# Two attentions that divide their values instead of their probabilities, and hand gated, split rows on

## The chip, the core and the metric

The kernel runs on one NeuronCore of a Trainium2 chip. The metric is the device time of one execution in microseconds (us), as the median of several runs. Its engines are PE (matmuls and transposes, into PSUM), DVE, ACT and POOL (elementwise work; POOL doesn't read PSUM here) and SP, whose queue issues most DMAs. Each engine runs its own list in order; they meet through semaphores and wait for one another at the end of each block.

## What is computed

The program is a first transformer block (latent attention, differential attention, routed experts), which the change doesn't touch, and a second block of two layers on a sequence of 1024 with width 1024 and 16 heads of 64. Cut to its two attentions:

```python
# layer 1: forgetting attention
logits = q @ k.T * scale + c[:, None] - c[None, :]        # c: running sum of log forget gates
p = softmax(where(causal, logits, -inf))
o = p @ v
h = h + (o * silu(gate)) @ w_out_a
# layer 2: window of 128 keys, 4 key/value heads, one sink logit a head
probs = softmax(concatenate([logits, sink], -1))[..., :-1]
o = probs @ v_band
h = h + (o * silu(gate)) @ w_out_b
```

All is f32. The output projections are made of three f32r products of split operands: x = hi + lo, x_hi is the cast of x to f32r, x_lo = x - x_hi, and hi·hi + hi·lo + lo·hi is summed (`split_product`, lines 329 to 331).

## The kernel before

Memory is a row of 16 KiB slots; a name such as `oh_a` or `wo_a` is a tile at a slot, and `_rest` is the low part, written over its source.

**First attention (`phase_fox`, 64 pairs).** A pair p is a pair of heads c = p // 8 and a query tile t = p % 8 of 128 rows; its keys are the t + 1 tiles up to the diagonal. So a pair's cost grows with t and starts over every eight pairs. PE's list has in step p: transposes of the probabilities of pair p-3 (first four key tiles), a mask matmul and the scores of pair p, the value product of pair p-4, and the remaining transposes of pair p-3 (only for t of 4 and more). DVE adds the gate row C and takes the maximum (L2531), ACT does exp with the row sum (L2492), DVE the reciprocal (L2539), POOL multiplies every probability in place by the reciprocal (L2503), and then PE may transpose (L2562). The transposed tiles go from PSUM to `fox_pt`: the first four key tiles by ACT (L2480), the rest by DVE (L2517), through three PSUM banks in turn. The value product (L2601) writes a quarter of bank 7, transposed: head dimension down, queries across. ACT copies the bank to `qa` (L2486) after every fourth pair, and the product of the next pair waits for that.

**Output projection (`phase_gated_out`).** It begins after a barrier. For the first layer SP loads both halves of the weights, `wo_a`, and then H; for the second they were loaded during the attention. DVE multiplies the attention output by the gate G in eight pieces of 1024 columns (L2682), ACT casts it (L2659), DVE subtracts (L2686). ACT casts the weights (L2657, L2663), POOL subtracts the first half (L2674), DVE the second (L2691). PE waits for four output pieces and a whole weight half, then runs 16 units of 24 matmuls; DVE adds each to H (L2700).

**Window attention (`phase_window`, 32 units).** A unit is one key/value head j, of four query heads, and one query tile b; b = 0 has half the keys. PE in step u: mask (L3146) and scores (L3151) of unit u, transposes of u-3 (L3163), value product of u-4 (L3175). DVE: maximum (L3116) and four small operations, reciprocal (L3126), and both copies of transposed tiles (L3134, L3135). ACT: four exps (L3088) and the copy of the values to `qb` (L3096). POOL scales the probabilities (L3075).

## Time and profile before

| | us |
|---|---|
| median of 3 runs (2932.11 to 2933.54) | 2932.21 |
| the profiled execution | 2931.2 |
| its span in the trace | 2929.0 |

| engine | busy us | share of the span |
|---|---|---|
| PE | 2510.2 | 86% |
| DVE | 1702.3 | 58% |
| ACT | 1353.0 | 46% |
| POOL | 639.6 | 22% |

In the profile times are from the start of the span. The first attention runs from 1997.8 to 2295.6, its output projection until about 2414, the window attention from 2686.2 to 2816.9, the last projection to the end. A matmul's record ends some 0.27 us after PE could issue the next (the drain); an idle time in brackets stands ahead of the row, with what ended it; "x20" counts merged instructions. An f32 matmul that isn't a transpose has two records.

### The profile page before, as it was taken

Reading aid. Unit: us, or ns where it says so; the run is one execution under the profiler, and the core shown is the slowest. Engines: PE = TensorE matmul, PEld = TensorE weight load, DVE = VectorE, ACT = ScalarE, POOL = GpSimd, SP = SyncE. Lnnn points to the kernel's source line nnn. Section 1 sums busy time; section 2 is a strip of 40 time slices with the busy share of each in tenths; the row PEclk is TensorE's granted clock in tenths of the full one; section 3 lists DMA queues with packets and bytes.
Section 4 is the critical chain, followed back from the end, with each engine's and each line's share of the span. In section 5 each row is a group of like instructions: output and inputs, shape, how many; then the busy total and the mean of one; then the engine's idle time right before and its main releaser. Section 6 shows DMA issues by size and latency. Waiting matters only on the chain. (4 is left out here: it accounts for less than half of the span.)

```text
span 2929.0 us, 37676 instructions
## 1 busy us (share of the span) xinstructions
PE 2510.2 (86%) x13381; PEld 2013.9 (69%) x13381; DVE 1702.3 (58%) x2888; ACT 1353.0 (46%) x2358; POOL 639.6 (22%) x515
## 2 busy tenths in 40 slices
PE   1899799999975999999941999997888597998969
PEld 1787279788764888888831878885655476886547
DVE  5662655687336999999937145412444616742981
ACT  2243144696124888888834233323565304222540
POOL 0121012230101211111112000004777400002950
PEclk9899899999967999999975999998999798999989
DMA  6542000002027999999944211043000312114101
GB/s 221 173 129 62 0 1 1 1 30 87 0 74 323 409 415 417 412 412 410 410 161 179 78 44 59 22 137 115 30 30 16 116 58 87 29 47 156 57 8 51
DMA packets 126925, 400.22 MB, mean 137 GB/s; under 512 B 11947, under 2 KB 62256, under 8 KB 114370
## 3 DMA queue, kind: packets, MB, share of 16 engines
q1 hardware_dynamic: 113726, 354.07, 31.7%
q0 software_dynamic: 12048, 42.56, 3.7%
q8 instruction: 89, 1.46, 0.2%
q10 hardware_dynamic: 1012, 1.72, 0.2%
q14 instruction: 50, 0.41, 0.0%
HBM read 347.93 MB, written 50.40 MB: 136 GB/s over the span
## 5 line engine op out<-in xcount | busy, mean ns | idle before, releaser
L2503 POOL TENSOR_SCALAR fox_l<-fox_l,stat 128x256 f32<-128x256 f32 (+7 forms) x128 | 219.0, 1726 | 76.0 <-DVE stat L2539 76.0
L2531 DVE CUSTOM_DVE_ANT_0 fox_l<-PS,fox_c 128x256 f32<-128x256 f32 (+7 forms) x128 | 92.1, 756 | 156.3 <-PE PS L2585 111.2
L2492 ACT ACTIVATE fox_l<-fox_l,stat 128x256 f32<-128x256 f32 (+7 forms) x128 | 98.3, 770 | 75.3 <-DVE stat L2531 75.3
L3075 POOL TENSOR_SCALAR win_p<-win_p,stat 128x256 f32<-128x256 f32 (+1 forms) x128 | 110.7, 887 | 20.0 <-DVE stat L3126 20.0
L2562 PE MATMUL PS<-mats,fox_l 128*128 128x128 f32 x576 | 89.7, 291 | 25.8 <-POOL fox_l L2503 17.6
L329 PE MATMUL PS<-wehg,xsTh 128*128 128x512 f32 x256 | 100.4, 392 | 8.3 <-DVE we0g_rest L1888 6.9
L329 PE MATMUL PS<-wehd,aTh 128*128 128x512 f32 x256 | 100.5, 392 | 6.6 <-DVE aTl L1907 6.6
L329 PE MATMUL PS<-wqkh,uTh 128*128 128x512 f32 x256 | 103.3, 403 | 0.0
L329 PE MATMUL PS<-wehu,xsTh 128*128 128x512 f32 x256 | 102.9, 402 | 0.0
L331 PE MATMUL PS<-wqkh,uTl 128*128 128x512 f32 x256 | 100.5, 392 | 0.0
L331 PE MATMUL PS<-wehd,aTl 128*128 128x512 f32 x256 | 100.2, 391 | 0.0
L331 PE MATMUL PS<-wehg,xsTl 128*128 128x512 f32 x256 | 100.2, 391 | 0.0
L331 PE MATMUL PS<-wehu,xsTl 128*128 128x512 f32 x256 | 100.1, 391 | 0.0
L330 PE MATMUL PS<-wqk_rest,uTh 128*128 128x512 f32 x256 | 100.0, 391 | 0.0
L2562 PEld LDWEIGHTS PS<-mats,fox_l 128*128 128x128 f32 x576 | 64.3, 145 | 49.8 <-POOL fox_l L2503 40.6
L2700 DVE TENSOR_TENSOR H<-PS,H 128x512 f32<-128x512 f32 x32 | 21.9, 691 | 126.7 <-PE PS L331 126.6
L2601 PEld LDWEIGHTS PS<-fox_pt,va 128*64 128x64 f32 x1152 | 64.1, 140 | 39.4 <-ACT fox_pt L2480 36.4
L2601 PE MATMUL PS<-fox_pt,va 128*64 128x128 f32 x1152 | 79.9, 285 | 11.9 <-ACT qa L2486 10.9
L451 PE MATMUL PS<-mats,xn_na 128*128 128x128 f32 x64 | 11.5, 364 | 91.6 <-DVE xn_na L413 91.6
L1210 DVE TENSOR_REDUCE stat<-PS 128x1 f32<-128x1024 f32 x64 | 78.0, 1224 | 18.9 <-PE PS L1247 15.7
L329 PE MATMUL PS<-hTh,winh 128*128 128x512 f32 x208 | 83.2, 400 | 6.7 <-DVE win_rest L603 6.7
L2854 POOL DMA_DIRECT2D g_dram<-b_sg x16 | 8.7, 544 | 354.3 <-ACT b_sg L2909 354.3
(569 smaller groups left out, 7794.8 us busy)
## 6 DMA issues: line engine op xcount, KB each, us to landing
we0g<-in_w_expert_gate SPq DMA_DIRECT2D x16, 2048.0 KB, 11.1
we0u<-in_w_expert_up SPq DMA_DIRECT2D x16, 2048.0 KB, 9.6
we1g<-in_w_expert_gate SPq DMA_DIRECT2D x16, 2048.0 KB, 11.3
we0d<-in_w_expert_down SPq DMA_DIRECT2D x16, 2048.0 KB, 10.5
we1u<-in_w_expert_up SPq DMA_DIRECT2D x16, 2048.0 KB, 9.7
we1d<-in_w_expert_down SPq DMA_DIRECT2D x16, 2048.0 KB, 10.6
wada_rest<-in_w_ada SPq DMA_DIRECT2D x16, 1024.0 KB, 5.2
wada<-in_w_ada SPq DMA_DIRECT2D x4, 2048.0 KB, 13.5
```

The source lines that it names most:

```text
L329: nc.tensor.matmul(out, lh, rh, start=start, stop=False)
L330: nc.tensor.matmul(out, lh, rl, start=False, stop=False)
L331: return nc.tensor.matmul(out, ll, rh, start=False, stop=stop)
L451: last = nc.tensor.transpose(PS[:, u % NB, j * P:(j + 1) * P], xn[:, j, k * P:(k + 1) * P], env.ident)
L1210: nc.vector.reduce_max(nb[:, w % 4:w % 4 + 1], bank(w), AX_X, negate=True).then_inc(nb_ready, 1)
L2492: nc.scalar.activation(prob(p, e)[:, 0:K], prob(p, e)[:, 0:K], ACT.Exp, bias=nbm[:, u % 8:u % 8 + 1], scale=-1.0, accum_out=rsum[:, u % 8: ...
L2503: nc.gpsimd.tensor_scalar(prob(p, e)[:, 0:K], prob(p, e)[:, 0:K], rsum[:, u % 8:u % 8 + 1], None, ALU.mult).then_inc(p_ready, 1)
L2531: nc.vector.tensor_tensor_reduce(out=prob(p, e)[:, 0:K], in0=PS[:, 2 * e:2 * e + 2, :].rearrange("p a b -> p (a b)")[:, 0:K], in1=C[:, h % ...
L2562: last = nc.tensor.transpose(PS[:, 4 + at % NTB, (k % 4) * P:(k % 4 + 1) * P], prob(v, e)[:, k * P:(k + 1) * P], env.ident)
L2601: last = nc.tensor.matmul(PS[e * HD:(e + 1) * HD, 7, (t % 4) * P:(t % 4 + 1) * P], env.va[:, k, h * HD:(h + 1) * HD], PT[:, w % 2, e, k, : ...
L2700: nc.vector.tensor_tensor(H[:, t, h], PS[:, u % 8, :], H[:, t, h], ALU.add).then_inc(h_done, 1)
L3075: last = nc.gpsimd.tensor_scalar(p, p, rs[:, c + i:c + i + 1], None, ALU.mult)
```

## The change

It does three things in both attentions. First, probabilities are transposed and multiplied with the values undivided. POOL instead copies the two (window: four) reciprocals of a pair over 64 columns a head (`rx`), PE transposes this tile, and it lands in the same PSUM bank beside the value sums, laid out as they are; DVE multiplies the two. In the first attention it first copies the turned reciprocals to SBUF, and does this for two pairs at once, after every odd pair; in the window it first multiplies them by the gate. Second, the gate, the cast and the subtraction of the attention output move from the projection into the attention, onto POOL (window: the gate onto DVE). Third, the projection takes ready rows. The first half of `wo_a` is loaded while the first attention runs, all weight casts are ACT's and all weight subtractions DVE's, and PE waits for weight pieces one by one. In the window the copies of transposed tiles go from DVE to ACT, as one instruction, and ACT's copy of the values goes away. G of the window comes in four loads.

```diff
+    nbm, rsum = env.stat[:, 0:8], env.stat[:, 8:24]
...
+    def rx(w):
+        at = (2 + w // 2 % 2) * P
+        return env.pad[w % 2][:, at:at + P]
...
+                if h == NH // 2 + 2:
+                    sp.wait_ge(s_ready, NPAIR)
+                    load(sp, env.wo_a[0:1])
...
-                w = p - LAG - 2
-                if w >= 0 and w % 4 == 3:
-                    c, n = w // T, w % T // 4
-                    act.wait_ge(pv_done, w + 1)
-                    nc.scalar.copy(env.qa[:, c, n * HALF:(n + 1) * HALF], PS[:, 7, :]).then_inc(o_out, 1)
...
-            for p in range(NPAIR if scale_on_pool else 0):
...
+            for p in range(NPAIR + LAG + 2):
+                if p < NPAIR:
+                    at = 2 * p % 16
                     pool.wait_ge(r_ready, p + 1)
-                    nc.gpsimd.tensor_scalar(prob(p, e)[:, 0:K], prob(p, e)[:, 0:K], rsum[:, u % 8:u % 8 + 1], None,
-                                            ALU.mult).then_inc(p_ready, 1)
+                    if p >= 4:
+                        pool.wait_ge(pv_done, p - 3)
+                    nc.gpsimd.tensor_copy(rx(p).rearrange("p (e d) -> p e d", e=2),
+                                          rsum[:, at:at + 2].unsqueeze(2).to_broadcast([P, 2, HD])
+                                          ).then_inc(rx_ready, 1)
+                w = p - LAG - 2
+                if w < 0 or w % 2 == 0:
+                    continue
+                i = w // 2
+                o = two(env.qa, w)
+                if i == 0:
+                    pool.wait_ge(g_in, 16)
+                pool.wait_ge(o_out, i + 1)
+                nc.gpsimd.tensor_tensor(o, o, two(g, w), ALU.mult).then_inc(gated, 1)
+                pool.wait_ge(gated, i + 1)
+                nc.gpsimd.tensor_copy(two(Oh, w), o).then_inc(o_hi, 1)
+                pool.wait_ge(o_hi, i + 1)
+                nc.gpsimd.tensor_tensor(two(Ol, w), o, two(Oh, w).bitcast(F32), ALU.subtract).then_inc(o_lo, 1)
...
-            for p in range(NPAIR + LAG + 1):
+            for p in range(NPAIR + LAG + 2):
+                w = p - LAG - 2
+                if w >= 0 and w % 2:
+                    rb = env.pad[w // 2 % 2][:, 0:2 * P]
+                    dve.wait_ge(pv_done, w + 1)
+                    if w >= 4:
+                        dve.wait_ge(o_out, w // 2 - 1)
+                    nc.vector.tensor_copy(rb, PS[:, 7, 2 * P:4 * P]).then_inc(rb_out, 1)
+                    dve.wait_ge(rb_out, w // 2 + 1)
+                    nc.vector.tensor_tensor(two(env.qa, w), PS[:, 7, 0:2 * P], rb, ALU.mult).then_inc(o_out, 1)
...
-                    pe.wait_ge(p_ready, 2 * v + e + 1)
+                    pe.wait_ge(exp_done, 2 * v + e + 1)
...
+                    pe.wait_ge(rx_ready, w + 1)
+                    if w >= 2:
+                        pe.wait_ge(o_out, w // 2)
+                    nc.tensor.transpose(PS[:, 7, (2 + w % 2) * P:(3 + w % 2) * P], rx(w), env.ident)
                     pe.wait_ge(pt_first, 2 * w + 2)
...
-                    if w >= 4:
-                        pe.wait_ge(o_out, w // 4)
...
-                            last = nc.tensor.matmul(PS[e * HD:(e + 1) * HD, 7, (t % 4) * P:(t % 4 + 1) * P],
+                            last = nc.tensor.matmul(PS[e * HD:(e + 1) * HD, 7, (w % 2) * P:(w % 2 + 1) * P],
...
-            load(sp, wo_loads)
+            load(sp, loads)
...
+            for j in range(8):
+                act.wait_ge(wo[j // 4][1], 16)
+                nc.scalar.copy(wpiece(woh, j), wpiece(raw, j)).then_inc(w_hi, 1)
...
-            for j in range(4):
...
+            for j in range(8):
                 dve.wait_ge(w_hi, j + 1)
...
+                nc.vector.tensor_tensor(wpiece(wl, j), wpiece(raw, j), wpiece(woh, j).bitcast(F32), ALU.subtract
+                                        ).then_inc(w_lo, 1)
...
-                if n == 0:
-                    pe.wait_ge(o_lo, 4 * (t // 4) + 4)
...
-                pe.wait_ge(w_lo2 if n else w_lo, 4)
+                    if t == 0 and k % 2 == 0:
+                        pe.wait_ge(w_lo, 4 * n + k // 2 + 1)
...
+            for j in range(KVH):
+                sp.dma_start(g[:, 2 * j:2 * j + 2, :], env.g_dram.rearrange("(k p) s -> p k s", p=P)[:, 2 * j:2 * j + 2, :]
+                             ).then_inc(g_in[j], 16)
+            load(sp, env.wo_b)
...
-            for v in range(NU):
-                f = first(units[v][1])
-                pool.wait_ge(r_ready, v + 1)
-                for i in range(G):
-                    p = Pb[:, v % 4, i, f:]
-                    last = nc.gpsimd.tensor_scalar(p, p, rs[:, c + i:c + i + 1], None, ALU.mult)
-                last.then_inc(p_ready, 1)
+            for u in range(NU + 5):
+                if u < NU:
+                    at = 4 * (u % 8)
+                    pool.wait_ge(r_ready, u + 1)
+                    if u >= 2:
+                        pool.wait_ge(o_ready, u - 1)
+                    nc.gpsimd.tensor_copy(rx(u).rearrange("p (c e d) -> p c e d", c=2, e=2),
+                                          rs[:, at:at + 4].rearrange("p (e c) -> p c e", e=2).unsqueeze(3)
+                                          .to_broadcast([P, 2, 2, HD])).then_inc(rx_ready, 1)
+                w = u - 5
+                if w >= 0:
+                    pool.wait_ge(o_out, w + 1)
+                    nc.gpsimd.tensor_copy(block_of(Oh, w), block_of(env.qb, w)).then_inc(o_hi, 1)
+                    pool.wait_ge(o_hi, w + 1)
+                    nc.gpsimd.tensor_tensor(block_of(Ol, w), block_of(env.qb, w), block_of(Oh, w).bitcast(F32),
+                                            ALU.subtract).then_inc(o_lo, 1)
...
+                v = u - 3
+                if v >= 0:
+                    f = 1 if units[v][1] == 0 else 0
+                    act.wait_ge(t_ready, v + 1)
+                    if v >= 2:
+                        act.wait_ge(o_ready, v - 1)
+                    nc.scalar.copy(PT[v % 2][:, f:, :], PS[:, 4 + f:6, :]).then_inc(pt_ready, 1)
...
-                w = u - 4
-                if w >= 0:
-                    act.wait_ge(o_ready, w + 1)
-                    nc.scalar.copy(env.qb[:, 2 * j:2 * j + 2, b * P:(b + 1) * P],
-                                   PS[:, 6 + w % 2, 0:2 * P].rearrange("p (c q) -> p c q", c=2)).then_inc(oo_act, 1)
...
-                        dve.wait_ge(o_ready, v - 1)
-                    if units[v][1]:
-                        nc.vector.tensor_copy(PT[v % 2][:, 0, :], PS[:, 4, :])
-                    nc.vector.tensor_copy(PT[v % 2][:, 1, :], PS[:, 5, :]).then_inc(pt_dve, 1)
...
+                w = u - 5
+                if w >= 0:
+                    dve.wait_ge(o_ready, w + 1)
+                    if w % T == 0:
+                        dve.wait_ge(g_in[w // T], 16)
+                    do(nc.vector.tensor_tensor(rg(w), PS[:, 6 + w % 2, 2 * P:4 * P].rearrange("p (c q) -> p c q", c=2),
+                                               block_of(g, w), ALU.mult))
+                    nc.vector.tensor_tensor(block_of(env.qb, w),
+                                            PS[:, 6 + w % 2, 0:2 * P].rearrange("p (c q) -> p c q", c=2), rg(w), ALU.mult
+                                            ).then_inc(o_out, 1)
...
-                    pe.wait_ge(p_ready, v + 1)
+                    pe.wait_ge(exp_done, v + 1)
-                        pe.wait_ge(pt_dve, v)
+                        pe.wait_ge(pt_ready, v)
...
+                    pe.wait_ge(rx_ready, w + 1)
+                    if w >= 2:
+                        pe.wait_ge(o_out, w - 1)
+                    for c in range(2):
+                        nc.tensor.transpose(PS[:, 6 + w % 2, (2 + c) * P:(3 + c) * P], rx(w)[:, c * P:(c + 1) * P], env.ident)
+                    pe.wait_ge(pt_ready, w + 1)
...
+    env.G, env.O_a = gates("a", 3), (m.at("oh_a", 3, [P, KD, S], F32R), m.rest("qa"))
+    env.wo_a = out_weights("a", (7, 9), A["w_out_a_2"][0])
...
+    phase_gated_out(nc, A, env, sem, "a", env.O_a, env.wo_a, env.wo_a[1:], (8, 10), H, sem("h_in_a"),
+                    env.h_dram, [env.ha_dram], extra=trig)
...
+    env.Gb, env.Gb_in = m.at("G_b", 3, [P, KD, S]), [sem(f"G_in_b{j}") for j in range(KVH)]
+    env.wo_b, env.h_in_b = out_weights("b", (5, 6), A["w_out_b_2"][0]), sem("h_in_b")
+    env.O_b = m.at("oh_b", 3, [P, KD, S], F32R), m.rest("qb")
...
+    phase_gated_out(nc, A, env, sem, "b", env.O_b, env.wo_b, [], (7, 8), H, env.h_in_b, None, [out])
```

## Rows read from the trace of the kernel before

**Rows 1.** Busy time by stretch: us, PE, PEld, DVE, ACT, POOL, clock, DMA
```profile
1997.80:2295.60 297.80, 249.89 (x2240) 171.12 (x2240) 125.53 (x384) 168.62 (x401) 219.05 (x128) 0.95 0.12 44
...
2686.20:2816.90 130.70, 113.69 (x800) 65.92 (x800) 111.80 (x284) 72.96 (x320) 110.67 (x128) 0.98 0.26 97
```

**Rows 2.** Waits in the first attention: engine, releaser, us, times, longest
```profile
DVE fox_l L2531 <- PE PS L2585: 111.2, 56, 2.9
...
PEld PS L2562 <- POOL fox_l L2503: 40.6, 58, 1.8
...
PE PS L2601 <- ACT qa L2486: 10.9, 8, 1.8
```

**Rows 3.** Timeline of one head pair: the mask matmul opening a score step
```profile
2102.30 0.28 PE L2579 MATMUL PS<-masksb,identb 128*128 128x128 bf16 x2
...
2107.18 0.28 PE L2579 MATMUL PS<-masksb,identb 128*128 128x128 bf16 x2
...
2112.82 0.28 PE L2579 MATMUL PS<-masksb,identb 128*128 128x128 bf16 x2
...
2117.22 0.28 PE L2579 MATMUL PS<-masksb,identb 128*128 128x128 bf16 x2
...
2132.21 0.28 PE L2579 MATMUL PS<-masksb,identb 128*128 128x128 bf16 x2
...
2137.69 0.28 PE L2579 MATMUL PS<-masksb,identb 128*128 128x128 bf16 x2
```

**Rows 4.** Timeline, same pair: what PE waited for, and a releasing copy
```profile
2104.29 1.31 PE L2601 MATMUL PS<-fox_pt,va 128*64 128x128 f32 x20 [1.30 <-ACT qa L2486]
...
2112.33 0.66 PE L2562 MATMUL PS<-mats,fox_l 128*128 128x128 f32 x4 [1.54 <-POOL fox_l L2503]
...
2136.80 0.47 DVE L2517 COPY fox_pt<-PS 128x128 f32<-128x128 f32 x2
...
2137.22 0.63 PE L2562 MATMUL PS<-mats,fox_l 128*128 128x128 f32 x4 [0.99 <-DVE fox_pt L2517]
```

**Rows 5.** Timeline at the end of the first attention
```profile
2278.52 10.67 POOL L2503 TENSOR_SCALAR fox_l<-fox_l,stat 128x896 f32<-128x896 f32 x4 [0.44 <-DVE stat L2539]
...
2295.59 0.59 ACT L2486 COPY qa<-PS 128x512 f32<-128x512 f32 x1 [5.07 <-PE PS L2601]
```

**Rows 6.** Groups by form, first attention: count, busy us, mean ns
```profile
L2531 DVE CUSTOM_DVE_ANT_0 fox_l<-PS,fox_c 128x256 f32<-128x256 f32 x16 | 6.2, 423 | 11.5 <-PE PS L2585 11.5
```

**Rows 7.** Timeline from the first attention into its output projection
```profile
2296.49 2.36 DVE L2682 TENSOR_TENSOR qa<-qa,G_a 128x1024 f32<-128x1024 f32 x2 [3.00 <-PEq L2458]
...
2306.28 1.04 ACT L2657 CAST woh_a<-wo_a 128x1024 fp32r<-128x1024 f32 x1 [10.10 <-DMA wo_a<-in_w_out_a]
...
2310.77 3.36 DVE L2682 TENSOR_TENSOR qa<-qa,G_a 128x1024 f32<-128x1024 f32 x1
...
2324.16 0.80 PE L329 MATMUL PS<-woh_a,oh_a 128*128 128x512 f32 x1 [28.60 <-DVE qa_rest L2686]
...
2332.04 4.62 DVE L2691 TENSOR_TENSOR wo_a_rest<-wo_a,woh_a 128x1024 fp32r<-128x1024 f32 x4
```

**Rows 8.** Timeline of POOL in an earlier stage: a cast, a two-input pass
```profile
510.15 1.04 POOL L959 CAST dif_kh<-dk 64x1024 fp32r<-64x1024 f32 x1 [11.57 <-ACT dif_kh L987]
511.27 2.35 POOL L961 TENSOR_TENSOR dif_kz<-dk,dif_kh 64x1024 fp32r<-64x1024 f32 x1
```

**Rows 9.** Second attention: three mask matmuls; ACT's and DVE's forms
```profile
2740.39 0.60 PE L3146 MATMUL PS<-masksb,identb 128*128 128x512 bf16 x2
...
2744.03 0.39 PE L3146 MATMUL PS<-masksb,identb 128*128 128x256 bf16 x2
...
2774.55 0.39 PE L3146 MATMUL PS<-masksb,identb 128*128 128x256 bf16 x2
...
L3088 ACT ACTIVATE win_p<-PS,stat 128x256 f32<-128x256 f32 x112 | 51.6, 473 | 44.0 <-DVE stat L3120 44.0
...
L3135 DVE COPY win_pt<-PS 128x512 f32<-128x512 f32 x32 | 21.7, 679 | 0.0
```

**Rows 10.** Timeline: the second output projection's first matmul
```profile
2836.60 0.79 PE L329 MATMUL PS<-woh_b,oh_b 128*128 128x512 f32 x1 [19.71 <-DVE qb_rest L2686]
```

More of the change, by code:

```diff
@@ L2467, in _ @@
                     load(sp, [env.G])
+                if h == NH // 2 + 2:
+                    sp.wait_ge(s_ready, NPAIR)
+                    load(sp, env.wo_a[0:1])
         @block.scalar
         def _(act):
-            for p in range(NPAIR + LAG + 2):
+            for p in range(NPAIR + LAG):
                 v = p - LAG
@@ L2653, in _ @@
         def _(act):
-            for i in range(NP_):
-                if i < 4:
-                    act.wait_ge(halves[0][1], 16)
-                    nc.scalar.copy(wpiece(woh, i), wpiece([x[0] for x in halves], i)).then_inc(w_hi, 1)
-                act.wait_ge(gated, i + 1)
-                nc.scalar.copy(piece(Oh, i), piece(O, i)).then_inc(o_hi, 1)
-            act.wait_ge(halves[1][1], 16)
-            for j in range(4, 8):
-                nc.scalar.copy(wpiece(woh, j), wpiece([x[0] for x in halves], j)).then_inc(w_hi, 1)
+            for j in range(8):
+                act.wait_ge(wo[j // 4][1], 16)
+                nc.scalar.copy(wpiece(woh, j), wpiece(raw, j)).then_inc(w_hi, 1)
             if extra is not None:
@@ L3053, in four, with rx, rg, block_of @@
         return PS[:, 2 * (u % 2):2 * (u % 2) + 2, :].rearrange("p a (i k) -> p (a i) k", i=2)
[L3055 to L3057 removed]
+    def rx(w):
+        return env.pad[w % 2][:, 2 * P:4 * P]
+    def rg(w):
+        return env.pad[w % 2][:, 0:2 * P].rearrange("p (c q) -> p c q", c=2)
+    def block_of(x, w):
+        j, b = units[w]
+        return x[:, 2 * j:2 * j + 2, b * P:(b + 1) * P]
     with nc.Block() as block:
@@ L3104, in do @@
                 dve.wait_ge(dve_step, step.mark(instruction))
-            for u in range(NU + 3):
+            for u in range(NU + 5):
                 if u < NU:
@@ L3207, in second_block @@
     del taken[:]
-    env.G = gates("a", 3)
+    env.c_in = [sem(f"c_in{i}") for i in range(4)]
+    env.C = m.at("fox_c", 11, [P, 4, S])
+    env.G, env.O_a = gates("a", 3), (m.at("oh_a", 3, [P, KD, S], F32R), m.rest("qa"))
+    env.wo_a = out_weights("a", (7, 9), A["w_out_a_2"][0])
     phase_fox(nc, A, env, sem)
```

130 lines of the change are left out of this document (41 added, 89 removed).

## The prediction

> **What bounds the kernel now.** I began with the busy time in stretches [rows 1]. The change touches two attention stages and the hand-over from each to its output projection, and these differ in kind. In the first attention (297.8 us) PE is busy for 249.9 us by modelled ends, POOL for 219.1 and no engine is full. The waits there [rows 2] show PE held for POOL, which scales every probability tile in place ahead of its transposes, and for ACT's evacuation of the value sums. In the 28.6 us behind it PE does nothing at all [rows 7]. The second attention has POOL busy for 110.7 of 130.7 us and PE for 113.7; behind it lies another gap of 19.7 us [rows 10]. So each part has to be read by itself: a loop of dependences, a plain gap, a nearly full PE, and a second gap.
>
> **First hand-over, the largest term.** ACT's last evacuation starts at 2295.59, just as the last value product ends [rows 5]; the first projection matmul starts at 2324.16 after 28.60 us of idle PE [rows 7]. Between them lie the wait for the weights (the first cast starts at 2306.28, 10.10 us of it on the DMA), then gating, casting and subtracting of the whole attention output. POOL subtracts the weights at the same time; DVE's product takes 3.36 us then. In the new kernel the first weight half is in SBUF already and the output rows are gated and split inside the attention. What is left behind the last value product is:
> - DVE copies 256 columns of turned reciprocals out of PSUM and multiplies. The nearest row is a DVE pass over 256 PSUM columns, 0.423 us [rows 6]; two of them and a semaphore step are 0.9.
> - POOL gates, casts and subtracts 256 columns. POOL's two-input pass over 1024 columns takes 2.35 us and its cast 1.04 [rows 8]. By columns that is 0.6 + 0.26 + 0.6; with 0.1 a step for start and semaphore I take 1.9. The bounds are 1.5 (by columns) and 5.7 (the full 1024-column prices).
> - The barrier between blocks: ACT's last copy ends at 2296.18 and DVE starts the next block at 2296.49, 0.3 [rows 5, 7].
> - The first piece of weights: a cast of 1.04 us, then a DVE subtraction, four of which take 4.62 us [rows 7]. With its semaphore steps this is 2.5.
>
> Together 5.6 us in place of 28.6: **-23 us**. Later pieces come every 1.2 us, and PE needs at least 1.4 us for the six matmuls of a piece, so it isn't starved. The new load of the second half is wanted only eight units later: the 16 additions to H of this block follow PE, not the load. PE started out of a long idle stretch before too, so I book nothing for its clock.
>
> **Second hand-over.** The gap is 19.71 us [rows 10]. The new tail is shorter, since DVE gates here: 0.9 (DVE), a cast and a subtraction of 256 columns on POOL, 1.1, then 0.3 and 2.5 as above: 4.8. **-15 us**.
>
> **First attention's loop.** Its period is one pair of heads: 2102.30 to 2137.69, 35.39 us, repeated [rows 3]. I walk it by the starts of the mask matmuls, each of which opens a score step. PE issues in order, so the step length is what stood in its way:
> - Step t=0, 4.88 us. The value product at 2104.29 had waited 1.30 us for ACT's copy of a full bank [rows 4]. That wait goes, and 0.29 us for POOL; one more transpose is added. The transposes that follow one another run at 0.11 us each (four of them read 0.66 us with the drain of 0.27 [rows 4]). About 3.4.
> - Step 1, 5.64 us. PE stood 1.54 us for POOL at 2112.33 [rows 4]. Without it DVE's new copy and product, 0.9 us, stand ahead of the second PSUM evacuation that frees the transposes' bank. So the gain is 1.5 and not 1.9 with the ACT wait: 4.1.
> - Step 2, 4.40 us: its product waited 0.55 us behind the late transposes; with one transpose more, 4.0.
> - Steps 3 to 6, 14.99 us together [rows 3]. These are set by scores, then DVE's logits pass, then the next scores, and DVE has 1 to 2 us of slack in them for its new pair. 14.9.
> - Step 7, 5.48 us, gets **longer**. DVE finishes the longest logits pass, and its copy at 2136.80 is what releases PE at 2137.22 (0.99 us of wait) [rows 4]. The new copy and product stand in front of it in DVE's queue: 5.5 + 0.9 = 6.4.
>
> Sum 32.8, that is 2.6 less for each of seven periods: -18. The first period has no POOL wait to lose but gets the 0.9, +0.6. The drain was ruled by POOL, which had 10.67 us of scaling still queued at 2278.52 [rows 5]; following the same queues without it I get the last product 3 us sooner. **-20.5** in all. Unknown here is the order in which DVE's new pair meets its waits. If it costs 0.9 at every even step instead of two, four times eight, the gain is 20.5 - 14 = 6. If it hides everywhere, it is 20.5 + 14 = 34; steps 3 to 6 give nothing either way.
>
> POOL's work in this loop falls from 27 us in a period to about 10: eight broadcast copies of 128 columns and four chains of three instructions. The broadcast copies are needed three steps later. POOL's wait on the gate chain holds only the next such copy, with that slack. The added waits on `pv_done` are for a buffer last used four pairs earlier. The SP queue stops at head 10 until half the scores are done; behind it is the row of head 11, wanted one period (33 us) later, and the 2 MB weight load ahead of it took 10 us in [rows 7]. I book nothing.
>
> **Second attention's loop.** Period of eight units: 2744.03 to 2774.55, 30.52 us [rows 9]. A step in which PE waits for nothing is 3.64 us (2740.39 to 2744.03). Eight of these, less 1.5 for the first block with half the keys, are 27.6: PE idles 2.9. Two added transposes a unit, 0.22, give 29.3. ACT gives up its 0.38 us copy of the values and takes DVE's two copies as one of 1024 columns: about 1.0 with four exponentials of 0.47 and their accumulator reads [rows 9] makes 3.1 a unit, under 3.7. DVE, at 111.8 / 32 = 3.5 us a unit [rows 1], loses two copies of 0.68 [rows 9] and gains 0.9. So PE is the bound and the gain is 30.5 - 29.4 = 1.1 for each of three periods, -3.4, and 2 us in the drain, where POOL and DVE no longer stand between the last transposes and their products: **-5.4**. Bounds: +4 if each pair of transposes also costs a drain of 0.17 and the old idle time stays, -9 if the idle time goes in the first period too.
>
> **Sum.** 23 + 15 + 20.5 + 5.4 = 64 us. The profiled execution took 2931.2 us (its span 2929.0 and 2.2 around it), 1.0 under the median of 2932.2. 2931.2 - 64 = 2867, and about 2868 by the median.
>
> **Rivals.**
> 1. *DVE becomes the link in the first loop.* The new copy and product lengthen every even step, and what POOL's waits gave is taken back: -6 instead of -20.5. For it: step 7 shows that DVE's copies do release PE. Against: in steps 4 and 6 DVE waits for PE (111 us over the stage [rows 2]). Time 2868 + 14.5 = 2883; 2889 if nothing at all is left.
> 2. *The transposes cost more in the window stage.* PE is nearly full there, so an added switch or a late reciprocal goes straight through: +4 instead of -5.4, time 2878.
> 3. *DVE slack in the first loop is larger than I read*, and the new pair hides at steps 1 and 7 too: 2868 - 14 = 2854.
> 4. *Slower than before: POOL and DVE exclude one another.* A DVE pass with both inputs in SBUF takes 1.2 us by itself (four in 4.62) and took 3.36 beside a POOL subtraction [rows 7]. In the window stage DVE has some 3.1 us of work a unit and POOL 2.0; run strictly one after the other, with 0.1 us for each of nine semaphore steps, they make 6.0 us a unit against 3.8. That is 32 x 2.2 = +70, and with it the 5.4 isn't gained: 2931 - 64 + 5 + 70 = 2942. It turns slower from 5.8 us a unit on. Against it: the first attention's DVE passes over PSUM keep their length (0.423 us mean over 16) with POOL busy almost all the time [rows 6, 1].
>
> The Trainium skill, "SBUF — State Buffer", section "Who interferes with whom", calls the shared ports an exclusive lock, but says that a DVE instruction with at most one SBUF input, outside the two-port modes, doesn't contend with GpSimd; both new DVE passes read PSUM for the other input, so by that rule rival 4 falls away, and by the lock taken without the exception it would stand. The rows of the first attention agree with the exception.
>
> **How the numbers follow.** Forecast 0.62 (2860 to 2876); rival 1, 0.18; rival 2, 0.08; rival 3, 0.07; rival 4, 0.05. The likeliest is 2868. For 8 in 10 the range takes in rivals 1 to 3 and their combination, 2851 to 2894, leaving out rival 4 and the far tails. A measurement can tell 0.2%, 6 us, from no change. All cases but rival 4 are faster by far more: faster 0.94, within 0.2% 0.01, slower 0.05.
>
> **What would show each step.** The PE idle ahead of the first matmul of each projection: near 5.6 and 4.8 us, released by a DVE subtraction of weights and not by one of attention rows. The period of the first loop near 33 us, with step 7 near 6.4 and no wait of PE on POOL's scaling; if it is 35, rival 1. The window's period near 29.4, PE's idle under 0.5 a unit. POOL's three new instructions of 256 columns at 0.7, 0.3 and 0.7 us; over 1.5 each would say rival 4. The prediction fails most cheaply in the hand-overs: if the projection's first matmul waits on something I took as ready (the barrier behind POOL, the weight half, a queue of POOL's gates that is units behind), each microsecond there counts in full.

## The result, and the profile after

The changed kernel takes 2877.54 us (2876.0 to 2881.6), against 2932.88 us for the kernel before on the same chips: a ratio of 0.9815, with a 95% interval of 0.9803 to 0.9826. That is 55 us less, where 64 had been worked out. Its profiled execution has a span of 2875.5 us, 53.5 less than before.

I cut both spans at the same six events (first mask matmul and last value product of each attention, first matmul of each output projection) and take differences:

| part | worked out | measured |
|---|---|---|
| first hand-over (PE idle) | 28.60 to 5.6: -23 | 28.60 to 5.68: -22.9 |
| second hand-over | 19.71 to 4.8: -15 | 19.71 to 6.47: -13.2 |
| first attention, loop and drain | -20.5 | -10.9 |
| second attention, loop and drain | -5.4 | -7.4 |
| all that lies ahead of, between and behind | 0 | +1.0 |
| sum | -64 | -53.4 |

The 1.0 is 1.2 us by which the first attention starts later, behind code that the change doesn't touch. In the other kernels below that start lies anywhere from 1997.3 to 2003.1 us, so differences of a few us between whole runs are read by stages, not by spans.

Busy time of the changed kernel by stretch, columns as in [rows 1]: first attention, first gap, second attention, second gap.
```profile
1999.06:2285.83 286.77, 259.60 (x2304) 174.84 (x2304) 149.22 (x446) 163.11 (x385) 75.03 (x157) 0.96 0.15 53
2285.83:2291.50 5.67, 0.00 (x0) 0.00 (x1) 2.13 (x4) 2.36 (x3) 3.68 (x6) 0.78 0.19 42
2653.36:2776.58 123.22, 120.02 (x864) 72.86 (x864) 89.21 (x286) 94.47 (x321) 43.77 (x90) 0.98 0.27 103
2776.58:2783.05 6.47, 0.01 (x1) 0.00 (x0) 2.12 (x4) 2.35 (x3) 3.55 (x7) 0.81 0.00 0
```
POOL's busy time falls from 219 to 75 us in the first attention. In the second PE is now busy for 120.0 of 123.2 us.

The first hand-over, timeline of all engines from the last value product to the first projection matmul. It answers to [rows 7].
```profile
2285.86 0.42 DVE L2539 COPY pad<-PS 128x256 f32<-128x256 f32 x1 [2.15 <-PE PS L2629]
2286.32 0.42 DVE L2541 TENSOR_TENSOR qa<-PS,pad 128x256 f32<-128x256 f32 x1
2286.82 0.72 POOL L2524 TENSOR_TENSOR qa<-qa,G_a 128x256 f32<-128x256 f32 x1 [5.97 <-DVE qa L2541]
2287.61 0.40 POOL L2526 CAST oh_a<-qa 128x256 fp32r<-128x256 f32 x1
2288.09 0.72 POOL L2528 TENSOR_TENSOR qa_rest<-qa,oh_a 128x256 fp32r<-128x256 f32 x1
2289.14 3.88 ACT L2674 CAST woh_a<-wo_a 128x1024 fp32r<-128x1024 f32 x4 [8.52 <-PEq L2469]
...
2290.22 2.36 DVE L2687 TENSOR_TENSOR wo_a_rest<-wo_a,woh_a 128x1024 fp32r<-128x1024 f32 x2 [3.48 <-ACT woh_a L2674]
...
2291.50 0.79 PE L329 MATMUL PS<-woh_a,oh_a 128*128 128x512 f32 x1 [5.68 <-DVE wo_a_rest L2687]
```
This is the chain of the prediction, link by link: 0.9 us on DVE, 2.0 on POOL (1.9 had been taken), 0.3 for the barrier, 2.4 for the first piece of weights. ACT finds the weights landed.

One period of the first loop, PE's timeline, cut to the mask matmuls that open steps 0 to 4, step 7 and the next period, and to what PE waited for. It answers to [rows 3, 4].
```profile
2101.99 0.27 PE L2605 MATMUL PS<-masksb,identb 128*128 128x128 bf16 x2
2102.19 0.49 PE L2611 MATMUL PS<-ka,qa 64*128 64x128 f32 x4
2102.61 0.33 PE L2622 MATMUL PS<-mats,pad 128*128 128x128 f32 x1
2102.87 1.31 PE L2629 MATMUL PS<-fox_pt,va 128*64 128x128 f32 x20
...
2105.62 0.28 PE L2605 MATMUL PS<-masksb,identb 128*128 128x128 bf16 x2
...
2109.79 0.63 PE L2588 MATMUL PS<-mats,fox_l 128*128 128x128 f32 x4 [0.30 <-DVE fox_pt L2550]
2110.26 0.28 PE L2605 MATMUL PS<-masksb,identb 128*128 128x128 bf16 x2
...
2114.91 0.28 PE L2605 MATMUL PS<-masksb,identb 128*128 128x128 bf16 x2
...
2118.83 0.28 PE L2605 MATMUL PS<-masksb,identb 128*128 128x128 bf16 x2
...
2129.95 0.28 PE L2605 MATMUL PS<-masksb,identb 128*128 128x128 bf16 x2
...
2135.76 0.63 PE L2588 MATMUL PS<-mats,fox_l 128*128 128x128 f32 x4 [1.52 <-DVE fox_pt L2550]
2136.22 0.28 PE L2605 MATMUL PS<-masksb,identb 128*128 128x128 bf16 x2
```
The period is 34.23 us, not 32.8. Behind the scores the transpose of reciprocals (L2622) starts at 2102.61 and the value product at 2102.87: 0.26 us for a transpose that had been priced at 0.11.

### The profile page after: what moved, and what is told of

Same layout as the page of the kernel before. It is cut to its first block and busy times, and to the rows that moved or that the text cites. A ratio compares the mean times of both kernels' runs of the same rounds, so it can differ in the third digit from the quotient of the medians.

```text
span 2875.5 us, 38066 instructions
## 1 busy us (share of the span) xinstructions
PE 2527.0 (88%) x13509; PEld 2023.6 (70%) x13509; DVE 1661.3 (58%) x2932; ACT 1351.2 (47%) x2326; POOL 409.7 (14%) x507
## 5 line engine op out<-in xcount | busy, mean ns | idle before, releaser
L2696 DVE TENSOR_TENSOR H<-PS,H 128x512 f32<-128x512 f32 x32 | 21.9, 691 | 130.7 <-PE PS L331 130.7
L1888 DVE TENSOR_TENSOR we1d_rest<-we1d,wehd 128x1024 fp32r<-128x1024 f32 x64 | 74.1, 1220 | 15.6 <-ACT wehd L1828 15.6
L2611 PE MATMUL PS<-ka,qa 64*128 64x512 f32 (+3 forms) x384 | 83.0, 538 | 0.0
L331 PE MATMUL PS<-hTh,win_rest 128*128 128x512 f32 x208 | 81.7, 393 | 0.0
L330 PE MATMUL PS<-hT_rest,winh 128*128 128x512 f32 x208 | 81.7, 393 | 0.0
L1888 DVE TENSOR_TENSOR we0d_rest<-we0d,wehd 128x1024 fp32r<-128x1024 f32 x64 | 74.1, 1220 | 9.7 <-ACT wehd L1828 9.7
## 6 DMA issues: line engine op xcount, KB each, us to landing
we1g<-in_w_expert_gate SPq DMA_DIRECT2D x16, 2048.0 KB, 10.9
wada<-in_w_ada SPq DMA_DIRECT2D x4, 2048.0 KB, 13.2
```

What stands on the lines that cost most here:

```text
L330: nc.tensor.matmul(out, lh, rl, start=False, stop=False)
L331: return nc.tensor.matmul(out, ll, rh, start=False, stop=stop)
L1888: nc.vector.tensor_tensor(piece(wl[j][kind], kind, i), piece(w[j][kind], kind, i), piece(wh[kind], kind, i).bitcast(F32), ALU.subtract).th ...
L2611: last = nc.tensor.matmul(PS[:, 2 * e + n, 0:N], env.qa[r, c, t * P:(t + 1) * P], env.ka[r, c, n * HALF:n * HALF + N], start=(n != d), sto ...
L2696: nc.vector.tensor_tensor(H[:, t, h], PS[:, u % 8, :], H[:, t, h], ALU.add).then_inc(h_done, 1)
```

## Experiments

Each kernel is told by its edit. PE's stretch from the first mask matmul to the first projection matmul (before: 326.3 us, changed kernel: 292.4) is given where the edit is in the first attention, since it leaves out what varies ahead of it.

**Only the second attention and its projection changed (window_only).** The edit puts the new `phase_window`, a projection that takes split rows and the loads by KV head into the kernel before.

> The kernel before with the second attention and the last output projection of the changed kernel; the first attention and its projection stay as they were. Theory (the two halves of the change are independent, as the traces read: window stage -7.4 us, second hand-over -13.2): 20.6 us under the kernel before, ratio 0.9930, and the remaining 34 us belong to the first attention and its hand-over. Rival (they share something, a clock level or the start of the second norm): more than 3 us off that sum.

Measured: 2912.0 us, ratio 0.9925 (0.9909 to 0.9942), 20.4 us under the kernel before. The first gap is 28.61 us, as before, the window stage's first to last mask matmul 110.44 us, as in the changed kernel. The halves add up (20.6 had been expected), and about 35 us belong to the first. Its first attention is that of the kernel before; its stretch to the first projection matmul is 327.6 us, 1.3 longer, with one step 0 of 6.94 us, of which more under before_unscaled.

**Load of the first weight half left in the projection (late_load).**
```diff
-                if h == NH // 2 + 2:
-                    sp.wait_ge(s_ready, NPAIR)
-                    load(sp, env.wo_a[0:1])
...
-    phase_gated_out(nc, A, env, sem, "a", env.O_a, env.wo_a, env.wo_a[1:], (8, 10), H, ...
+    phase_gated_out(nc, A, env, sem, "a", env.O_a, env.wo_a, env.wo_a, (8, 10), H, ...
```

> The changed kernel with one edit undone: the first half of the output weights of the first attention is loaded when the projection's block starts, not during the attention. Theory (hand-over is a chain: weights land, cast, subtraction, first matmul): about 10 us slower than the changed kernel, some 2887.5 us, since before the change ACT waited 10.10 us for these weights; of the 22.9 us of the first hand-over 10 are then the load and 13 the gating and splitting of rows. Rival (the load is mostly hidden by the barrier and by the gating tail): under 3 us slower.

Measured: 2886.1 us, ratio 0.9845 (0.9829 to 0.9862), 8.6 us slower than the changed kernel; the stretch to the first projection matmul is 302.4 us, 10.0 longer. From its timeline:
```profile
2287.25 1.01 SPq L322 DMA_DIRECT2D wo_a<-in_w_out_a  x2
...
2297.38 3.89 ACT L2671 CAST woh_a<-wo_a 128x1024 fp32r<-128x1024 f32 x4 [18.64 <-DMA wo_a<-in_w_out_a]
2298.46 4.63 DVE L2684 TENSOR_TENSOR wo_a_rest<-wo_a,woh_a 128x1024 fp32r<-128x1024 f32 x4 [13.60 <-ACT woh_a L2671]
...
2299.74 0.80 PE L329 MATMUL PS<-woh_a,oh_a 128*128 128x512 f32 x1 [15.80 <-DVE wo_a_rest L2684]
```
From issue to cast are 10.1 us, and the gap is 15.80 instead of 5.68. So of the 22.9 us 10.1 come from the early load, given that the rows are ready; the other 12.8 belong to the rest of the change together. No run takes that rest apart, nor tries the early load alone in the kernel before, where PE waited for rows and not for weights. The trace of the kernel before says where most of the 12.8 lay. POOL subtracted weights there beside DVE's passes over the rows; the second row is one of DVE's passes once POOL is done:
```profile
2307.41 12.20 POOL L2674 TENSOR_TENSOR wo_a_rest<-wo_a,woh_a 128x1024 fp32r<-128x1024 f32 x4 [8.36 <-ACT woh_a L2657]
...
2322.89 1.21 DVE L2686 TENSOR_TENSOR qa_rest<-qa,oh_a 128x1024 fp32r<-128x1024 f32 x1
```
DVE's four passes in POOL's 12.20 us took 2.54, 3.36, 3.37 and 3.35 us. At 1.21 each they would have been 7.8 us shorter (an estimate from these rows), and DVE, busy from 2308.31 on, was what PE waited for. Also, PE no longer waits for a whole weight half: in late_load the first of four pieces lets PE start 1.3 us after DVE begins, where all four take 4.63.

**The kernel before without POOL's scaling (before_unscaled).**
```diff
-            for p in range(NPAIR if scale_on_pool else 0):
+            for p in range(0):
...
-                    pe.wait_ge(p_ready, 2 * v + e + 1)
+                    pe.wait_ge(exp_done, 2 * v + e + 1)
```

> The kernel before with POOL's scaling of the probabilities in the first attention left out and nothing in its place (so that the values aren't divided there). Theory (by the prediction's steps): PE's 1.54 us at step 1 and 0.29 us at step 0 go, the wait of 1.30 us for ACT's full bank stays, period 35.39 to 33.6 us; with the drain about -16 us, 2916 us. Rival (POOL was only the last of several that came nearly together, the next one holds PE as long): period over 35 us, -3 us or less beyond the drain.

Measured: 2920.5 us, ratio 0.996 (0.9946 to 0.9974), -11.9 us and not -16; the stretch to the first projection matmul is 317.3 us, 9.0 shorter. The periods are of two kinds, 33.47 us (33.6 had been expected) and 34.79 us, in turn. The longer ones have a step 0 of 6.09 us in place of 4.75. Twenty matmuls of the same value product, in two periods that follow one another (first two rows), and the busy time of the three stretches around them (columns as in [rows 1]; the clock is the third number from the end):
```profile
2066.60 1.31 PE L2601 MATMUL PS<-fox_pt,va 128*64 128x128 f32 x20 [1.30 <-ACT qa L2486]
...
2100.07 2.40 PE L2601 MATMUL PS<-fox_pt,va 128*64 128x128 f32 x20 [1.29 <-ACT qa L2486]
```
```profile
2066.60:2069.00 2.40, 2.40 (x29) 2.07 (x30) 0.68 (x2) 0.65 (x5) 0.00 (x0) 1.00 0.60 241
...
2097.60:2100.00 2.40, 1.16 (x10) 0.86 (x10) 0.66 (x6) 2.40 (x6) 0.00 (x0) 0.93 0.78 169
2100.00:2102.40 2.40, 2.33 (x20) 2.03 (x21) 0.00 (x0) 0.69 (x4) 0.00 (x0) 0.50 0.68 268
```
PE's clock is at its lower level, 1.2 GHz, for 2.4 us there, after PE had stood still for 0.99 and again for 1.29 us. So the mechanism (POOL's waits are worth 1.9 us a period) stands, and a second one, not thought of, takes part of it back: four long steps, 1.3 us each. It was there in the kernel before. Two of its periods show the same long step 0 (6.22 and 6.21 us), but they keep their 35.39 us: PE waits for POOL in step 1 anyway, and the loss goes into that wait. In window_only, with the same first attention, four periods show it, and one of them (step 0 of 6.94 us) is 1.0 us longer as a whole. The drain gives nothing back: from the last mask matmul to the last value product's end it is 21.9 us, against 21.8 in the kernel before.

**Every transpose of reciprocals twice (rx_twice).**
```diff
-                    nc.tensor.transpose(PS[:, 7, (2 + w % 2) * P:(3 + w % 2) * P], rx(w), env.ident)
+                    for _ in range(2):
+                        nc.tensor.transpose(PS[:, 7, (2 + w % 2) * P:(3 + w % 2) * P], rx(w), env.ident)
...
-                    for c in range(2):
+                    for c in (0, 1, 0, 1):
```

> The changed kernel with every transpose of turned reciprocals issued twice (one more per pair of the first attention, two more per unit of the second). Theory A (0.26 us from that transpose to the value product is 0.11 for the transpose and 0.15 once, for going between matrices that use 64 rows, 128 rows and 64 columns): the second copy costs 0.11 us; +6 us in the first attention, +7 in the window stage, 2890 us. Theory B (such a transpose costs 0.26 us each by itself): +15 in the first, +7 to +16 in the second, 2900 to 2908 us.

Measured: 2886.8 us, ratio 0.9842 (0.9825 to 0.9858), +9.3 us. The pair of transposes and the product behind it:
```profile
2102.53 0.44 PE L2623 MATMUL PS<-mats,pad 128*128 128x128 f32 x2
2102.89 1.31 PE L2630 MATMUL PS<-fox_pt,va 128*64 128x128 f32 x20
```
0.36 us for two, where one took 0.26: the second costs 0.11, as theory A has it. Steps 0 to 3 are 0.11 us longer each, steps 4 to 7 take it up in DVE's shadow, so that the period is 34.68 us, +0.45, and the stretch to the first projection matmul 295.8 us, 3.3 longer and not 6: that steps 4 to 7 would hide it had not been reckoned with. The window stage is 6.0 us longer from first to last mask (7 had been expected); its full periods go from 29.36 to 31.12 us, 0.22 for two more transposes a unit.

**Reciprocals of two pairs transposed together (rx_pairs).**
```diff
-                    pe.wait_ge(rx_ready, w + 1)
-                    if w >= 2:
-                        pe.wait_ge(o_out, w // 2)
-                    nc.tensor.transpose(PS[:, 7, (2 + w % 2) * P:(3 + w % 2) * P], rx(w), env.ident)
+                    if w % 2 == 0:
+                        pe.wait_ge(rx_ready, w + 2)
+                        if w >= 2:
+                            pe.wait_ge(o_out, w // 2)
+                        for i in range(2):
+                            nc.tensor.transpose(PS[:, 7, (2 + i) * P:(3 + i) * P], rx(w + i), env.ident)
```

> The changed kernel with the turned reciprocals of two pairs transposed together at every even step of the first attention. Theory (the first such transpose behind the scores costs 0.26 us, one behind it 0.11): even steps 0 and 2 get 0.11 us longer, odd steps 1 and 3 0.26 shorter, steps 4 to 7 stay, since DVE sets them: period 34.23 to 33.9, -2.4 us. Rival (0.26 each): steps 0 and 2 get 0.26 longer and the period stays.

Measured in one run: steps 0 to 3 are 3.75, 4.37, 4.77 and 3.66 us (3.64, 4.63, 4.65, 3.92 in the changed kernel) and the period is 33.95 us, each step within 0.01 us of what was expected. But the second and third period have a step 0 of 5.22 and 5.03 us, and the stretch to the first projection matmul is 292.8 us, not shorter than the changed kernel's 292.4. The one run took 2879.1 us.

**Transposes of reciprocals left out (rx_first_only).** The edit puts `if w < 2:` ahead of the transpose.

> The changed kernel with the transposes of the reciprocals in the first attention left out from the third pair on (so that later rows are divided by the first pairs' sums); all else stays. Theory (0.26 us each at the steps that PE sets, nothing where DVE sets them): steps 0 to 3 0.26 us shorter each, step 7 and 4 to 6 the same: period 33.2 us, -8 us. Rival (steps 0 to 3 are set by DVE's copies): steps 1 and 2 keep their length, with the wait on DVE's copy longer by as much.

Measured: 2876.4 us in one run. Steps 0 to 3 are 3.38, 4.38, 4.40 and 3.66 us, 0.25 shorter each, and the undisturbed period is 33.21 us, as expected. Yet four of the periods have a step 0 of 4.81 to 4.94 us, and the stretch to the first projection matmul is 292.2 us, 0.2 shorter: next to nothing of the 8 us arrives. In one of them:
```profile
2099.93 0.71 PE L2588 MATMUL PS<-mats,fox_l 128*128 128x128 f32 x4 [1.78 <-DVE fox_pt L2550]
...
2101.51 2.39 PE L2630 MATMUL PS<-fox_pt,va 128*64 128x128 f32 x20
```
Twenty matmuls take 2.39 us instead of 1.31; the clock in the stretch 2100.4 to 2102.4 is 0.50.

**DVE's bank-freeing copies first (dve_order).** The block that copies the turned reciprocals and multiplies moves behind the block of second PSUM copies.
```diff
+                v = p - LAG - 1
+                if 0 <= v < NPAIR and v % T >= 4:
+                    ... (copies into PT, pt_second)
                 w = p - LAG - 2
                 if w >= 0 and w % 2:
...
                     nc.vector.tensor_tensor(two(env.qa, w), PS[:, 7, 0:2 * P], rb, ALU.mult).then_inc(o_out, 1)
-                v = p - LAG - 1
-                if 0 <= v < NPAIR and v % T >= 4:
```

> The changed kernel, with DVE's copies that free the transposes' bank put ahead of its new copy and product in the first attention. Theory (the new pair stands in front of what releases PE, by 0.84 us at step 7 and by 0.30 us at step 1): step 7 falls from 6.27 to about 5.45 us, step 1 from 4.63 to 4.3; period 34.23 to 33.1 us, eight of them -9 us, about 2868.5 us (0.3% under the changed kernel). Rival (the value product behind it waits for DVE's product instead): the time comes back at step 0 or 2, under 2 us gained.

Measured: 2867.2 us, ratio 0.9776 (0.9763 to 0.9789); this interval and that of the changed kernel (0.9803 to 0.9826) lie apart. The stretch to the first projection matmul is 284.0 us, 8.5 shorter (9 had been expected), and the period is 33.13 us. Step 7 of this kernel (its L2541 is the copy that frees the bank, L2550 and L2552 are the new pair):
```profile
2134.27 0.47 DVE L2541 COPY fox_pt<-PS 128x128 f32<-128x128 f32 x2
...
2134.65 0.42 DVE L2550 COPY pad<-PS 128x256 f32<-128x256 f32 x1
...
2134.68 0.63 PE L2588 MATMUL PS<-mats,fox_l 128*128 128x128 f32 x4 [0.73 <-DVE fox_pt L2541]
2135.10 0.42 DVE L2552 TENSOR_TENSOR qa<-PS,pad 128x256 f32<-128x256 f32 x1
```
PE waits 0.73 us instead of 1.52; step 7 is 5.49 us, step 1 4.31, and no later step gives it back. The pair's product isn't wanted before the transpose of reciprocals one step on.

**The same order, without the transposes (order_no_rx).** Both edits together.

> DVE's bank-freeing copies first, and the transposes of reciprocals in the first attention left out from the third pair on (later rows divided by the first pairs' sums). Theory (PE's clock falls at step 0 when PE has just stood still twice, at the end of step 7 and at the value product; with the stand at step 7 0.84 us shorter it doesn't): step 0 is 3.38 us in all periods after the second, period 33.13 - 1.05 = 32.1 us. Rival (less work on PE alone lets the clock fall): step 0 near 4.8 us in every second period, as in the kernel with the transposes left out alone.

Measured: 2861.4 us in one run; the period is 32.10 us, and from the second period on step 0 is 3.38 or 3.39 us each time. With PE's stand at step 7 shorter (0.99 us; 1.78 in rx_first_only) the clock holds, at the same work. It is one run of each.

**Three edits together (best1).** The order, the paired transposes, and in the second attention for the last six units:
```diff
-                    nc.gpsimd.tensor_copy(block_of(Oh, w), block_of(env.qb, w)).then_inc(o_hi, 1)
+                    if w < NU - 6:
+                        nc.gpsimd.tensor_copy(block_of(Oh, w), block_of(env.qb, w)).then_inc(o_hi, 1)
...
+                w = u - 5
+                if w >= NU - 6:
+                    act.wait_ge(o_out, w + 1)
+                    nc.scalar.copy(block_of(Oh, w), block_of(env.qb, w)).then_inc(o_hi2, 1)
```

> Three edits on the changed kernel: DVE's bank-freeing copies first, the turned reciprocals of two pairs transposed together at even steps, and in the second attention the casts of the last six units on ACT instead of POOL. Theory (the gains stand in different steps and add): period of the first loop 33.13 - 0.29 = 32.8 us, -2.3 us against the first edit alone, and the second gap 6.5 to 4.8 us, -1.7: 4 us under the 2867.2 us of the first edit, 2863 us. Rival (what shortens PE's work at step 0 to 3 lets its clock fall at step 0, as it did in two periods with the paired transposes alone and in four with most of them left out): some periods +1.3 us, the gain is gone, 2866 us or more.

Measured: 2866.9 us, ratio 0.9771 (0.9757 to 0.9784). The trace shows what was expected: period 32.83 us with no long step 0 after the first period, stretch to the first projection matmul 280.8 us (284.0 with the order alone), second gap 4.92 us. That is 4.7 us by stages (4 had been expected), but the medians of the two kernels differ by 0.3 us only, and their intervals overlap; whether it beats the order alone isn't shown. Both beat the changed kernel.

**The subtraction of the window's rows on DVE, one wait badly placed (dve_split).** POOL's subtraction of L3090 goes; DVE does it at the head of its turn u, for unit u - 7.

> The changed kernel with the subtraction of the second attention's rows (both inputs in SBUF) on DVE, not on POOL. This is the kind of DVE pass that rival 4 of the prediction is about. Theory (such a pass shares nothing with POOL's that costs): it takes about 0.33 us (a quarter of the 1.16 us of the 1024-column one and a start), period of the window stage stays near 29.4 us, and the second gap shrinks by POOL's backlog of 1.7 us. Rival (DVE's pass and POOL's exclude each other): passes beside POOL's copy and cast take 0.7 us and more.

Measured: 2941.3 us in one run, 64 us slower than the changed kernel and slower than the kernel before. The window stage goes from 110.4 to 164.3 us between its first and last mask matmul. DVE's pass takes 0.43 us, where 0.33 had been expected and the rival had 0.7 and more, and in all but the last few units it runs after POOL's work and not beside it, so the rival is hardly tested here. Four rows of one unit show what it is:
```profile
2722.47 0.41 PE L3194 MATMUL PS<-mats,pad 128*128 128x128 f32 x2 [1.88 <-DVE qb L3154]
...
2724.05 0.40 POOL L3082 COPY pad<-win_rs 128x256 f32<-128x256 f32 x1 [5.18 <-PE PS L3199]
...
2724.39 0.40 POOL L3088 CAST oh_b<-qb 128x256 fp32r<-128x256 f32 x1
...
2724.83 0.43 DVE L3125 TENSOR_TENSOR qb_rest<-qb,oh_b 128x256 fp32r<-128x256 f32 x1 [2.50 <-POOL oh_b L3088]
```
DVE's subtraction waits for POOL's cast. That cast stands in POOL's queue behind a broadcast copy, which waits for PE's newest value product to free its buffer. PE in turn waits for DVE's product of an earlier unit, which is queued behind DVE's next softmax work. The three engines take turns, 5.9 us a unit instead of 3.67.

**The same subtraction three units late (dve_split_late).** It stands ahead of L3153, DVE's gate product, for unit u - 8.

> The changed kernel with the subtraction of the second attention's rows on DVE, three units after the row is made, so that its operand was cast long before. It stands directly ahead of DVE's gate product and starts when POOL's broadcast copy starts, both being released by the same value product. Theory (no lock between two such passes): 0.43 us for DVE's, 0.40 for POOL's copy, the period stays at 29.4 us, the second gap shrinks by about 1.5 us: 2876 us. Rival (DVE with both inputs in SBUF and POOL exclude each other): one of the two becomes 0.3 us longer or starts that much later, each unit up to 0.3 us longer, +5 to +10 us.

Measured: 2878.1 us in one run (2876 had been expected); the unit is as long as in the changed kernel (first to last mask 110.45 us), the second gap is 5.12 us, 1.35 shorter (1.5 had been expected). A DVE pass with both inputs in SBUF beside POOL's copy:
```profile
2739.66 0.41 DVE L3148 TENSOR_TENSOR qb_rest<-qb,oh_b 128x256 fp32r<-128x256 f32 x1
2739.80 0.53 POOL L3082 COPY pad<-win_rs 128x256 f32<-128x256 f32 x1 [2.98 <-DVE win_rs L3141]
```
POOL's copy takes 0.53 us where it overlaps (0.40 elsewhere, 0.47 in the mean of 21). So the two do share something, for 0.13 us of an overlap of 0.27, and it costs the kernel nothing. The Trainium skill, "SBUF — State Buffer", section "Who interferes with whom", says that a DVE instruction with two SBUF inputs contends with a GpSimd instruction that reads SBUF; the row agrees as far as that. A lock held for DVE's whole pass, as the prediction quotes it, would have given 0.67 us instead of 0.53. What this run leaves out is a DVE pass of this kind beside a POOL subtraction, which is gone from POOL here; the numbers under late_load are of that pair, 3.36 us against 1.21 for 1024 columns.

## Why the prediction was right, and where it was off

**First hand-over: right to 0.1 us**, and for the reason given: late_load puts back 10.1 us, window_only all of the 28.6, and each link has its length. Nothing was booked for PE's clock, rightly: the first nine or ten matmuls of this projection start 0.43 us apart before they come to 0.23, after a stand of 5.68 us as after one of 28.60.

**Second hand-over: the mechanism right, POOL's term mis-sized.** 1.1 us was taken for a cast and a subtraction of the last unit alone. But POOL's last broadcast copies wait for value products, with the casts of finished units queued behind them. From 2773.44 us on POOL has six units to work off, one after the other, at 1.14 us each. Its last rows and DVE's last product:
```profile
2776.89 0.40 POOL L3088 CAST oh_b<-qb 128x256 fp32r<-128x256 f32 x1
2777.09 0.42 DVE L3152 TENSOR_TENSOR qb<-PS,pad 128x256 f32<-128x256 f32 x1
...
2779.65 0.72 POOL L3090 TENSOR_TENSOR qb_rest<-qb,oh_b 128x256 fp32r<-128x256 f32 x1
...
2783.05 0.80 PE L329 MATMUL PS<-woh_b,oh_b 128*128 128x512 f32 x1 [6.47 <-DVE wo_b_rest L2687]
```
DVE's last product ends at 2777.51, POOL's last subtraction at 2780.37: 2.9 us, 1.8 more than taken. With the casts on ACT the gap is 4.92 us. The prediction had named "a queue of POOL's gates that is units behind" as a way to fail, but its sum left it out.

**First attention: -10.9 instead of -20.5; this is the term that failed.** The removals were right: without POOL's scaling a period is 1.92 us shorter (before_unscaled; by 1.54 and 0.29 it had been 1.8), and the 1.30 us wait for ACT's full bank is gone. The additions were too small:

| step | before | predicted | after | what was missed |
|---|---|---|---|---|
| 0 | 4.88 | 3.4 | 3.64 | the transpose costs 0.26, not 0.11 |
| 1 | 5.64 | 4.1 | 4.63 | the transpose, and 0.30 of wait for DVE's copy |
| 2 | 4.40 | 4.0 | 4.65 | the 0.55 us was no wait of PE; the transpose |
| 3 to 6 | 14.99 | 14.9 | 15.04 | step 3 is set by PE and gets its 0.26 |
| 7 | 5.48 | 6.4 | 6.27 | nothing (dve_order gives 5.49) |

Three errors, then. First, the price of 0.11 us was read from transposes that follow one another, but this one stands alone between scores, which use 64 rows of the array, and the value product, which uses 64 columns. rx_twice and rx_pairs separate the two prices: 0.26 for the first, 0.11 for a second. The Trainium skill, "TensorEngine Tiling (Array Packing)", section "Key Properties", says that a change of tiling mode drains TensorE; the 0.15 us agree with that, and so does the window stage, where the added transposes stand behind other 128x128 ones and cost 0.11 each; no run here changes the shapes alone. Second, the 0.55 us at step 2 were idle time of PE's weight load while the scores still streamed (from the first score matmul to the next kind of matmul it is 0.84 us for 384 keys in both kernels), not of PE; the step has 4.40 us in before_unscaled too. The rows of the kernel before, weight load and matmul:
```profile
2113.87 1.51 PEld L2601 LDWEIGHTS PS<-fox_pt,va 128*64 128x64 f32 x28 [0.55 <-ACT fox_pt L2480]
2113.87 1.75 PE L2601 MATMUL PS<-fox_pt,va 128*64 128x128 f32 x28
```
Third, step 3 was put with the steps that DVE sets, while PE sets it. Together 1.43 us a period, 10 us in seven, which is the whole difference within 0.5 us. The first period came as worked out (+0.8, +0.6 taken).

**The drain: the number right, the mechanism not.** Counted from the last mask matmul it is 2.9 us shorter, where 3 had been taken on the ground that POOL's queued scaling ruled it. But before_unscaled has no scaling, and its drain is as long as before (21.9 us). The kernel before, where POOL held PE for 1.03 us only:
```profile
2281.21 2.40 PE L2601 MATMUL PS<-fox_pt,va 128*64 128x128 f32 x20 [1.83 <-ACT qa L2486]
...
2289.24 0.66 PE L2562 MATMUL PS<-mats,fox_l 128*128 128x128 f32 x4 [1.03 <-POOL fox_l L2503]
```
The larger items are the 1.83 us for ACT's full bank and the value product at the lower clock behind it, 2.40 us. The changed kernel has neither (its product takes 1.31), and pays for transposes and DVE's pair instead. That the sum came to 3 is luck.

Rival 1 (DVE becomes the link, -6) named one of the places, but not the sizes: DVE's pair costs 0.79 us at step 7 and 0.32 at step 1, as dve_order shows by taking 1.10 a period back, and nothing at the other even steps. The time lies between forecast and rival because PE itself got longer. Rival 3 is out, since the pair doesn't hide at steps 1 and 7.

**Window stage: -7.4 instead of -5.4, inside its bounds.** The period is 29.36 us (29.4 had been worked out), and PE is busy for all of it: a unit without a wait goes from 3.64 to 3.86 us, the 0.22 that had been booked. But of the three periods of the kernel before that the prediction took at 30.52 us the first is 29.89 (2714.14 to 2744.03). By periods the gain is 1.7, 0.5, 1.2 and, up to the last mask matmul, 1.4 us; the 1.7 in the first is what the lower bound had named. The drain gives 2.7, not 2. The upper bound of +4 doesn't follow from its own terms: 0.22 and 0.17 us in each of 32 units, less 2 in the drain, are about +10. Rival 2 is out by either.

**Rival 4 (POOL and DVE exclude one another) is out for this kernel.** DVE's two new passes, which read one input from PSUM, take 0.40 and 0.42 us with POOL at work beside them. With two SBUF inputs beside POOL's copy the price is 0.13 us (dve_split_late); beside a POOL subtraction it is the large one of [rows 7] (3.36 us against 1.21), and the changed kernel has no such pair of that size in its window stage. That dve_split lands at 2941 us, where the rival had 2942, is chance: the place is a wait in a queue, and the passes keep their length. The rival's turning point of 5.8 us a unit forgets the 5.4 us that it doesn't gain either; with them it is about 5.65.

**POOL's instructions** take 0.73, 0.40 and 0.73 us for 256 columns (0.7, 0.3 and 0.7 had been expected).

## What to carry to other kernels

A gap in which PE does nothing can be predicted by listing its links (here to 0.1 us), if each link is also asked what is queued ahead of it (here 1.7 us missed). A loop can't, unless every added instruction is priced in its place on its own engine, with the shapes of its neighbours. Put what frees another engine's buffer ahead of what is only wanted a step later: that order alone is worth 8.5 us of the first attention here. And of each wait in an in-order queue ask what stands ahead of the instruction that it waits for: the same pass one unit later costs nothing, one unit too early 64 us.

## What the runs showed of the hardware that I had not expected

- PE's clock falls to 1.2 GHz in single steps of a loop in which PE is busy most of the time. The value product of step 0 then takes up to 2.40 us instead of 1.31. Of the seven periods behind the first it did so in two of the kernel before, four of window_only (the same code there) and four of before_unscaled, each time after PE had stood still for 0.99 and 1.30 us just ahead; and in four of rx_first_only and two of rx_pairs, after 1.78 us. It did so in none with a stand of 1.52 us (the changed kernel), 1.41 (rx_twice), 0.99 alone (order_no_rx, best1) or 0.73 (dve_order). Why only some periods with the longer stands have it stays open. Where nothing else holds PE behind it, the step costs 1.3 to 1.6 us more.
- A single 128x128 transpose between scores and value product costs 0.26 us, the next one behind it 0.11, as do two behind other transposes in the window stage.
- POOL's copy of 256 columns goes from 0.40 to 0.53 us beside a DVE pass that reads two SBUF operands.
